# Combining the last expert blocks' outputs on the chip, with the rows of all other blocks read back while those blocks are still computed

## The reference

```
h2 = rmsnorm(x1)
coarse top-1 of 4 groups, then top-2 of 8 experts in it   -> two experts per token, weights w1, w2
y_k = (silu(h2 @ Wg[e_k]) * (h2 @ Wu[e_k])) @ Wd[e_k]      for k = 0, 1;  32 experts, hidden width 256
x  = x1 + w1*y_0 + w2*y_1
out = rmsnorm(x) * g_final
```

## Time and profile before

| | |
|---|---|
| median of 3 runs | 539.98 us |
| the profiled execution | 540.91 us |
| its span in the profile | 539.0 us |
| TensorE busy | 483.3 us (90%) |
| VectorE busy | 237.7 us (44%) |
| GpSimd busy | 183.3 us (34%) |
| ScalarE busy | 100.4 us (19%) |
| mean granted TensorE clock | 0.977 |
| read from HBM, written to HBM | 134.47 MB, 13.17 MB |

### The profile page before, as it was taken

How to read it: one execution, slowest core, us unless ns; L and a number is a source line. 1 busy time by engine, 2 the same in 40 slices (tenths; PEclk the granted TensorE clock), 3 DMA queues, 4 the chain that set the end, 5 groups by cost and what they waited for, 6 DMA issues and landing times.

```text
span 539.0 us, 8928 instructions
## 1 busy us (share of the span) xinstructions
PE 483.3 (90%) x3301; PEld 285.3 (53%) x3302; DVE 237.7 (44%) x514; ACT 100.4 (19%) x204; POOL 183.3 (34%) x282
## 2 busy tenths in 40 slices
PE   6999999999999999999679998989898982998884
PEld 3787777777777545545334443444443441443331
DVE  4219999999964422245821222222122210221246
ACT  5131011002104423324301111101111110011223
POOL 3010817647394600111234443333443332234101
PEclk9989999999999999999789999999999996999999
DMA  8995006100000597023959799999999999999477
GB/s 328 310 391 142 0 2 258 54 2 0 1 1 1 189 412 315 39 69 124 403 192 420 284 411 422 402 397 421 419 418 419 417 419 420 420 418 421 195 272 256
DMA packets 35509, 141.25 MB, mean 262 GB/s; under 512 B 10080, under 2 KB 10096, under 8 KB 23193
## 3 DMA queue, kind: packets, MB, share of 16 engines
q1 hardware_dynamic: 29194, 127.91, 60.4%
q0 software_dynamic: 4960, 9.45, 4.7%
q10 hardware_dynamic: 1327, 3.49, 1.8%
HBM read 134.47 MB, written 13.17 MB: 274 GB/s over the span
## 4 chain that ended last, share of the span: by engine, by line
PE 71%; DMA 12%; DVE 5%; issue 5%; SPq 3%; ACT 2%; POOL 1%; DVEq 0%; POOLq 0%; ACTq 0%
PE bank L1284 26%; PE bank L1367 10%; PE bank L1485 9%; PE bank L1505 8%; PE bank L1480 8%; DMA region_x<-in_w_up 5%; DMA region_w<-in_w_in 3%; PE bank L1277 2%; DMA slot<-y_rows 2%; SPq L402 2%; PE bank L1495 2%; PE bank L1433 1%; DVE ua L1169 1%; PE bank L1393 1%; DVE ua L1171 1%
## 5 line engine op out<-in xcount | busy, mean ns | idle before, releaser
L1284 PE MATMUL bank<-region_h,region_w 128*128 128x256 f32 (+1 forms) x576 | 142.3, 409 | 0.0
L1284 PEld LDWEIGHTS bank<-region_h,region_w 128*128 128x128 f32 x576 | 110.2, 192 | 30.5 <-issue 0.8
L1169 DVE TENSOR_TENSOR ua<-ua,bank 128x128 f32<-128x128 f32 x30 | 8.7, 288 | 174.2 <-ACT ua L639 174.2
L1367 PE MATMUL bank<-region_w,z 128*128 128x512 f32 x128 | 56.7, 596 | 0.2 <-ACT z L584 0.2
L1505 PE MATMUL bank<-region_w,ua 128*32 128x512 f32 x328 | 50.3, 598 | 3.3 <-DVE ua L1171 3.3
L928 DVE SCALAR_TENSOR_TENSOR z<-ub,par,z 128x512 f32<-128x512 f32 x60 | 48.7, 812 | 0.0
L928 DVE SCALAR_TENSOR_TENSOR region_x<-ub,par,region_x 128x512 f32<-128x512 f32 x56 | 45.9, 820 | 0.0
L1485 PE MATMUL bank<-region_w,z 128*32 128x256 f32 x512 | 45.1, 403 | 0.2 <-issue 0.2
L792 POOL COPY gcol<-gidx 128x1 uint32 (+1 forms) x30 | 5.4, 180 | 108.9 <-DVE sb_rows L1158 108.9
L723 POOL TENSOR_TENSOR ub<-region_x 128x512 f32<-128x512 f32 x4 | 20.2, 5056 | 63.8 <-ACT ub L538 32.6
L1485 PE MATMUL bank<-slot,z 128*32 128x256 f32 x192 | 25.9, 425 | 14.5 <-DMA region_w<-in_w_up 9.9
(11 more groups left out here) (244 smaller groups left out, 647.5 us busy)
## 6 DMA issues: line engine op xcount, KB each, us to landing
region_w<-in_w_down SPq DMA_DIRECT2D x21, 1024.0 KB
region_w<-in_w_gate SPq DMA_DIRECT2D x16, 1024.0 KB
region_w<-in_w_up SPq DMA_DIRECT2D x16, 1024.0 KB, 15.7
region_w<-in_w_in SPq DMA_DIRECT2D x4, 2048.0 KB, 19.5
slot<-in_w_gate SPq DMA_DIRECT2D x6, 1024.0 KB, 14.8
slot<-in_w_up SPq DMA_DIRECT2D x6, 1024.0 KB
slot<-in_w_down SPq DMA_DIRECT2D x6, 1024.0 KB
region_x<-in_w_up SPq DMA_DIRECT2D x5, 1024.0 KB
```

What stands on the lines that cost most here:

```text
L1284: ins = mm(ps[2 * bank + j][:, 0:LEN[j]], sec[name][:, k, c * P:(c + 1) * P], hT[:, k, CUT[j]], start=(k == 0), stop=(k == KC - 1))
L1367: ins = mm(ps[2 * (t % 2) + j][0:n, :], z[:, k, t * P:t * P + n], w_out_sb[:, k, j * 512:(j + 1) * 512], start=(k == order[0]), stop=(k == ...
```

## The change

- `y_rows` is filled with zeros by one DMA from a zeroed tile, in SP's queue behind the input weights; the loads of expert 0's gate and up move behind it and behind the router weights.
- `x1` is also stored to a new HBM tensor `x1_rows` (5 stores in SP's queue during the output projection), and the combination weights, transposed by TensorE, to `w_rows` (4 small DMAs of ScalarE).
- The last two blocks are not scattered. Their y stays in the two buffers `yblk`.
- SP no longer waits for all scatters before it loads `y_rows`: it waits for the scatters of all blocks but the last two, and for expert 27's last block (its slot, 3, and slot 2 now receive y). All tiles are then combined with what is there, tiles 1, 3 and 4 on TensorE and tiles 0 and 2 on VectorE, normalized and stored. Rows of the last two blocks' tokens are incomplete in this pass (a zero stands for their missing y).
- These at most 128 tokens are done a second time: GpSimd gathers their `x1` rows (`late`) and the y of their other expert (`other`), TensorE adds both and the two `yblk` buffers (each times a matrix of weights that routes rows to tokens, `same[b]`) in PSUM, ScalarE and VectorE normalize, and GpSimd scatters the rows over those in the outputs, after all plain stores have landed.
- The small tables for this (`vlast`, `ilast`, `dtok`) are computed on VectorE ahead of the block loop, the three gathers of weights (`wlate`) and the matrices `same`, `dother` around the last block. `keep_busy(24)` becomes 8 + 16 with the transpose between them; `keep_busy(32, 1)` is gone. For tiles on TensorE, ScalarE now takes 1024 columns at once, and GpSimd's part in their norm is gone.

The diff, cut to its core:

```diff
-BY_PE = (1, 3)
-
-FINISH = (0, 2, 1, 4, 3)
+BY_PE = (1, 3, 4)
+
+FINISH = (0, 1, 2, 3, 4)
...
+        x1_dram = nc.dram_tensor("x1_rows", (NTOK, D), fp32, kind="Internal").ap()
+
+        w_dram = nc.dram_tensor("w_rows", (2 * NTOK, 1), fp32, kind="Internal").ap()
...
-        yg = [[(SLOT0 if k == 0 else RW)[:, t * D:(t + 1) * D] for t in range(NT)] for k in range(2)]
+        zero = SLOT0[:, 0:D]
+
+
+        free = [RW[:, 2 * SEC + 3 * PART:2 * SEC + 6 * PART], RW[:, 0:3 * PART]]
+        yg = [[free[k][:, t * D:(t + 1) * D] for t in range(NT)] for k in range(2)]
+        late, other = [free[k][:, NT * D:(NT + 1) * D] for k in range(2)]
+        junk = z_t[:, 0:D]
...
+        FREE = 28
+        assert (FREE - 1) % NSLOT == 3 and FREE + NSLOT > NE
...
+        sums = [two_banks[2], two_banks[3], two_banks[1], two_banks[0]]
...
-            for part in range(2):
-                load_part(0, part, 0)
-
+
+            sp.wait_ge(s_zero, 1)
+            sp.dma_start(y_dram.rearrange("(i p) d -> p i d", p=P),
+                         zero.unsqueeze(1).to_broadcast([P, 2 * NTOK // P, D])).then_inc(s_yz, 16)
...
+            sp.wait_ge(s_yz, 16)
+            for part in range(2):
+                load_part(0, part, 0)
...
+            def store_x1(t):
+                sp.wait_ge(s_x1, 2 * t + 2)
+                sp.dma_start(x1_dram[t * P:t * P + TROWS[t], :], x1[0:TROWS[t], t, :]).then_inc(s_x1d, 16)
+
+            for t in range(NT - 1):
+                store_x1(t)
+
             sp.wait_ge(s_o, NT)
             load_expert(3, 3)
+            store_x1(NT - 1)
...
-            pairs = sp.value_load(bound[0:1, PAIRS:PAIRS + 1], min_val=NPAIR // 2, max_val=NBLK // 2)
+
+            lastp = sp.value_load(bound[0:1, LASTP:LASTP + 1], min_val=NPAIR // 2 - 1, max_val=NBLK // 2 - 1)
             odd = sp.value_load(bound[0:1, ODD:ODD + 1], min_val=0, max_val=1)
-            sp.wait_ge(s_ysc[1], pairs * 16)
-            sp.wait_ge(s_ysc[0], (pairs + odd) * 16)
-
-            for t, k in ((0, 0), (0, 1), (2, 0), (1, 0), (2, 1), (1, 1), (4, 0), (4, 1), (3, 0), (3, 1)):
-                sp.dma_start(yg[k][t][0:TROWS[t], :], y_dram[k * NTOK + t * P:k * NTOK + t * P + TROWS[t], :])\
-                  .then_inc(s_yg[k][t], 16)
+            done = sp.value_load(bound[0:1, FREE:FREE + 1], min_val=1, max_val=NBLK)
+            sp.wait_ge(s_ysc[1], lastp * 16)
+            sp.wait_ge(s_ysc[0], (lastp + odd) * 16)
+            sp.wait_ge(s_down, done)
+            for t in range(NT):
+                for k in range(2):
+                    sp.dma_start(yg[k][t][0:TROWS[t], :], y_dram[k * NTOK + t * P:k * NTOK + t * P + TROWS[t], :])\
+                      .then_inc(s_yg[k][t], 16)
...
+            act.wait_ge(s_wT, 1)
+            for k in range(2):
+                act.dma_start(w_dram[k * NTOK:k * NTOK + SEQ, :].rearrange("(t p) o -> t (p o)", p=P),
+                              wT[k * NT:(k + 1) * NT - 1, :]).then_inc(s_wd, 16)
+                act.dma_start(w_dram[k * NTOK + SEQ:(k + 1) * NTOK, :].rearrange("(t p) o -> t (p o)", t=1),
+                              wT[(k + 1) * NT - 1:(k + 1) * NT, 0:TROWS[NT - 1]]).then_inc(s_wd, 16)
...
+                if t == NT or t in BY_PE:
+                    i = len(BY_PE) if t == NT else BY_PE.index(t)
                     act.wait_ge(s_comb, i + 1)
-                    nc.scalar.activation(yg[0][t][:, 512:D], ps[5 + 2 * i][:, :], ACT.Square,
-                                         accum_out=small[:, 8 + t:9 + t]).then_inc(s_sqhalf, 1)
-                    nc.scalar.activation(yg[0][t][:, 0:512], ps[4 + 2 * i][:, :], ACT.Square,
-                                         accum_out=small[:, 16 + t:17 + t]).then_inc(s_sq3, 1)
-
-                    act.wait_ge(s_sq3, at + 1)
-                    act.wait_ge(s_eps3, i + 1)
-                    nc.scalar.activation(small[:, 40 + t:41 + t], small[:, 16 + t:17 + t], ACT.Sqrt,
-                                         scale=1.0 / D, bias=small[:, 48 + t:49 + t]).then_inc(s_rms3, 1)
-                    continue
-                act.wait_ge(s_fin, t // 2 + 1)
-                nc.scalar.activation(yg[0][t][0:n, :], x1[0:n, t, :], ACT.Square,
+                    src = sums[i][0:n, :]
+                else:
+                    act.wait_ge(s_fin, t // 2 + 1)
+                    src = x1[0:n, t, :]
+                nc.scalar.activation(junk[0:n, :], src, ACT.Square,
                                      accum_out=small[0:n, 16 + t:17 + t]).then_inc(s_sq3, 1)
...
+            pool.memset(zero, 0.0).then_inc(s_zero, 1)
...
+            pool.wait_ge(s_ilast, 7)
+            pool.wait_ge(s_wd, 64)
+            for i in range(3):
+                pool.indirect_dma_start(wlate[:, i:i + 1], None, w_dram[:, :],
+                                        bass.IndirectOffsetOnAxis(ap=ilast[:, 4 + i:5 + i], axis=0),
+                                        bounds_check=2 * NTOK - 1, oob_is_err=False).then_inc(s_wg, 16)
+            lastp = pool.value_load(bound[0:1, LASTP:LASTP + 1], min_val=NPAIR // 2 - 1, max_val=NBLK // 2 - 1)
+            done = pool.value_load(bound[0:1, FREE:FREE + 1], min_val=1, max_val=NBLK)
+            pool.wait_ge(s_x1d, 16 * NT)
+            for i in range(2):
+                pool.wait_ge(s_wexp[i][2], 16 * (NE // NSLOT + 1))
+
+            pool.wait_ge(s_yg[1][2], 16)
+            pool.wait_ge(s_down, done)
+            pool.wait_ge(s_ysc[1], lastp * 16)
+            pool.wait_ge(s_ysc[0], (lastp + odd) * 16)
+            pool.tensor_tensor(carry[:, 4:5], carry[:, 1:2], carry[:, 1:2], ALU.add)
+            pool.indirect_dma_start(late, None, x1_dram[:, :], bass.IndirectOffsetOnAxis(ap=ilast[:, 0:1], axis=0),
+                                    bounds_check=NTOK - 1, oob_is_err=True).then_inc(s_late, 16)
+            pool.indirect_dma_start(other, None, y_dram[:, :], bass.IndirectOffsetOnAxis(ap=ilast[:, 1:2], axis=0),
+                                    bounds_check=2 * NTOK - 1, oob_is_err=True).then_inc(s_late, 16)
+
+
+            pool.wait_ge(s_out, 16 * NT)
+            pool.wait_ge(s_nlate, 1)
+            for i, (dst, rows) in enumerate(((y_prompt[0], SEQ), (y_sample.rearrange("s l d -> (s l) d"), NS * SL))):
+                pool.indirect_dma_start(dst, bass.IndirectOffsetOnAxis(ap=ilast[:, 2 + i:3 + i], axis=0), late, None,
+                                        bounds_check=rows - 1, oob_is_err=False).then_inc(s_olate[i], 16)
...
-            link(nc.vector.tensor_tensor(w12[:, NT:2 * NT], w12[:, 0:NT], dlt, ALU.mult))
+            nc.vector.tensor_tensor(w12[:, NT:2 * NT], w12[:, 0:NT], dlt, ALU.mult).then_inc(s_w12, 1)
+            dve.wait_ge(s_wT_ps, 1)
+            nc.vector.tensor_copy(wT, ps[6][0:2 * NT, 0:P]).then_inc(s_wT, 1)
...
+                    nc.vector.tensor_scalar(diag[i][k], ident[0:n, 0:n], w12[0:n, k * NT + t:k * NT + t + 1], None,
...
+            dve.wait_ge(s_yc, 1)
+            even, uneven = pairs * 2 + odd * 2 - 2, pairs * 2 - 1
+            nc.vector.tensor_copy(vlast[:, 0:1], sidx[:, bass.ds(even, 1)])
+            nc.vector.tensor_copy(vlast[:, 1:2], sidx[:, bass.ds(uneven, 1)])
+            nc.vector.tensor_copy(vlast[0:T, 2:3], sidx[0:T, bass.ds(even, 1)])
+            link(nc.vector.tensor_copy(vlast[T:P, 2:3], sidx[T:P, bass.ds(uneven, 1)]))
...
+            nc.vector.tensor_scalar(dtok, ident[:, :], token, float(DA), ALU.mult, ALU.mult).then_inc(s_dtok, 1)
...
+            dve.wait_ge(s_trow, 1)
+            dve.wait_ge(s_wg, 48)
+            for b in range(2):
+                nc.vector.tensor_scalar(same[b], ps[6][:, 0:P], vlast[:, 3 + b:4 + b], wlate[:, b:b + 1],
+                                        ALU.is_equal, ALU.mult).then_inc(s_same, 1)
+            nc.vector.tensor_scalar(dother, ident[:, :], wlate[:, 2:3], None, ALU.mult).then_inc(s_same, 1)
...
-            keep_busy(24)
+            keep_busy(8)
+            pe.wait_ge(s_w12, 1)
+            tr(ps[6][0:2 * NT, 0:P], w12, ident[:, :]).then_inc(s_wT_ps, 1)
+            keep_busy(16)
...
+            pe.wait_ge(s_dtok, 1)
+            mm(ps[6][:, 0:P], lnmean[:, :], dtok, start=True, stop=True).then_inc(s_trow, 1)
...
+                if i == 1:
+                    pe.wait_ge(s_same, 3)
+                if i == 2:
+                    pe.wait_ge(s_yc, pairs * 2 + odd + 1)
+                    mm(sums[i][0:32, 0:1], onesb[:, 0:32], onesb[:, 0:1], start=True, stop=True)
                 for j in range(2):
-                    mm(ps[4 + 2 * i + j][:, :], ident[:, :], x1[:, t, j * 512:(j + 1) * 512], start=True, stop=False)
-            keep_busy(32, 1)
-            for i, t in enumerate(BY_PE):
+                    mm(sums[i][0:n, j * 512:(j + 1) * 512], ident[0:n, 0:n], x1[0:n, t, j * 512:(j + 1) * 512],
+                       start=True, stop=False)
                 for k in range(2):
                     pe.wait_ge(s_yg[k][t], 16)
                     for j in range(2):
```

(38 more changed lines are left out.)

80 lines of the change are left out of this document (45 added, 35 removed).

## The result

The changed kernel takes 551.83 us (median of 4 runs, 549.29 to 554.11), the kernel before 539.82 us beside it (537.75 to 540.32): ratio 1.0229, 95% interval 1.0171 to 1.0286. The prediction was 534.7, faster, with a range of 530.8 to 538.8. It was wrong in sign. The profiled execution took 553.13 us, its span is 551.1. Times here are medians and ratios of executions in the fast state; two far from all others (2699 us in e4, 823 us in the kernel before beside e9 to e12) are left out.

The account below looks back on a forecast made before the run. Bound by scatter, load, combine in series at the end. Loads 10.1 us earlier, half given back: 532.9, plus 0.6 front and 0.2 waits, 533.7, 5.3 below 539.0; 539.98 - 5.3 = 534.7, range 530.8 to 538.8.

Parts of the forecast that it names:

- What bounds the kernel now: End of kernel: scatter, load, combine in series, 27.2 us, with some 10 us of idle DMA ahead of y's loads.
- The front: Start through block 0: zeros, x1 stores and tables nearly all hidden; +0.6 us, for tile 4's x1 store.
- When y can be loaded: SP's queue: block 27's scatter lands about 504.0, first y load at 504.1 instead of 514.24, 10.1 us earlier.
- The engines at the end: Combining the tiles: VectorE and loads set the pace, two 0.46 us matmuls per y load; TensorE finishes tile 4 by 519.9.
- Rival (4): Combine at the end: TensorE at 1.2 GHz, 26 matmuls at 0.93 us, late sum to 534.6, median 543.9; chance 0.05.
- The late rows: Second pass for the last two blocks' tokens: gathers landed 521.5, 8 matmuls of 3.7 us, late sum done 525.2.
- rival (1): Late path: gathers and scatters slower under load, late rows at 523.6, scatters 1 us more; +3, 537.7; chance 0.15.
- Behind the late sum: From late sum at 525.2: ScalarE 526.7, VectorE 528.3, scatters landed 532.4, end 532.9 before front and Pool waits.

Follow-up runs that it names:

- e4: Kernel after without late gathers, late sum, its norm and late scatters (a probe, result incomplete): 536.24 us, ratio to the kernel before 0.9966.
- e9: Kernel after with combine calls on 256 columns, not 512 (half not summed), plus bf16 filler matmuls ahead of TensorE's waits: 546.67 us, ratio to the kernel before 1.0121.
- e12: Kernel before with only the change's front (zeros, order of first loads, stores of x1): ratio to the kernel before 1.0000.
- e1: Kernel after with tile 4's sum put back on VectorE: 552.33 us, ratio to the kernel before 1.0270.
- e6: Kernel before with one small GpSimd memset at the end, waiting for the last tile's norm: ratio to the kernel before 1.0049.
- e2: Kernel after with the four products of yblk done ahead of tile 1's sum: 546.55 us, ratio to the kernel before 1.0170.
- e5: Kernel after with every combine call on 256 columns in place of 512, half not summed: 551.18 us, ratio to the kernel before 1.0218.
- e7: Kernel before with norms of TensorE's tiles 1024 columns wide, without two small GpSimd instructions: ratio to the kernel before 0.9994.
- e11: Kernel after with e1 and e2, ident products early, late gathers right after block 27's y, late sum before tile 3, tile 4 before 3: 546.26 us, ratio 1.0107.

## Why the prediction was wrong

**What bounds the kernel now, The front, When y can be loaded**: right. The scatter of block 27 landed at 504.14 (504.0 forecast), the first load was issued at 504.30. The idle 10 us of DMA were there to be had. The landings were not: the first came at 507.82 (507.7 forecast), the next five 1.7 to 2.5 late, tile 3's second y at 521.84 (517.5) and tile 4's at 523.02 (518.9). Each load lands in 16 parts. The last part was late; the first parts kept a pace of 1.3 us, near the forecast 1.4. From the first issue to the last landing the ten loads took 18.7 us, 15.8 in the kernel before. The late gathers are not the cause: in e4, without them, it is 18.8. SP's ten loads took, from issue to landing (min/median/max), in the kernel after and then in the kernel before:

```profile
DMA to landing us min/median/max: 3.5/9.1/13.3
```

```profile
DMA to landing us min/median/max: 3.5/8.0/11.1
```

**The engines at the end: the step that failed.** I wrote "two matmuls of 0.46 per y load, from 3.70 for 8". The row is right and the reading wrong: its 8 instructions are 4 calls, two tiles by two halves, as the loop at L1557 says. A y load is two calls and four instructions, 1.86 us. The Trainium skill, "FP8 and Floating Point Precision", section "TensorE Precision Notes", has true fp32 go through the array four times; an estimate from that is 4 x 512 columns at 2.4 GHz, 0.85 us a call, and the trace agrees, with 0.86 to 0.93. So the combine was never "VectorE and the loads set this": 26 calls are 24 us of TensorE. Tile 3 was done at 525.9 (518.5 forecast), tile 4 at 531.3 (519.9). Rival (4) had this price, "26 matmuls at 0.93 us", and I gave it 0.05, since I took 0.93 for the price at 1.2 GHz. It is the price at 2.4. Its condition, the end at 1.2 GHz, did not come about, so the rival was near for a wrong reason; its late sum ended at 534.6, 4.5 too early, by the late y and the clock.

**The late rows.** Forecast 525.2, measured 539.1, 13.9 us later, and the parts add up: both gathers had landed at 528.8 and not 521.5, 7.3; TensorE reached them 2.5 later, at 531.3; 16 instructions took 7.8 with the one before them and not 3.7, 4.1. Of the 2.5, 1.7 is the clock in 520 to 525. The gathers are the second term that was too small: the first was issued at 518.57 (515.4 forecast), and from there to the landing of both it took 10.2 us and not 6.1; rival (1) had them at 523.6. The two errors hide each other. With gathers on time TensorE would still have come at 531.3 and ended at 539.1; with the forecast's TensorE, the gathers alone would have put the end at 532.5 (528.8 and 3.7). e1 shows the same from the other side: without the 2.5 the gathers decide, and the clock gives most of the time back. In e9, with the work that the forecast charged and the clock held, the late sum ended 21.9 us after the copy in place of 28.7; the forecast, 525.2, is 14.7 after it in the kernel before. So TensorE's price and its clock are worth 6.8 us, and of the 7.2 that are left 6.5 are the gathers' (17.5 us after the copy, 11.0 by the forecast's 521.5).

**Behind the late sum.** Forecast 7.9 us, measured 12.0. ScalarE, VectorE and the scatters were near their prices (scatters 2.3 to 2.6 from issue to landing), and 4.1 is the drain, for which there was no term. The kernel before had its drain level with SP's end (538.8 both), so its cost was invisible, and "the kernel ends when the last store has landed" held there only just. e6 shows that a later last instruction of GpSimd moves the end; in the kernel after SP was through at 546.9, 4.0 ahead of the drain's end. With these 13.9 and 4.1 more, and the front's 0.6 less, the forecast's 533.7 becomes the span of 551.1.

**What was really on offer.** Half of it I had seen: that the late part is a second combination in series. e4 puts the gain from the early loads at 1.8 us (0 to 3.6 by its interval) even with no late part at all, since TensorE's three tiles are then what ends last (its sum of tile 4 ends at 529.35, the last store lands at 535.2, the span at 535.7). The change pays 13.7 us for it. The 1.8 is no bound on what early loads can give: e4 with tile 4 on VectorE and the clock held was not run.

Open: why the runs of e2 and e9 fall into two groups of mean clock; why the clock stayed low in e5 beside a busy TensorE; and what spreads the landings of the last y loads (with e4, not the late gathers).

## What to carry to other kernels

Divide the xN of a profile's matmul group by the calls in the source before taking a price from it; fp32 is two instructions a call here. Check what stands level with the end (GpSimd's drain, a second wait) before you make the last step one of GpSimd's, and ask of every wait that you add on TensorE what clock the work behind it will get. Where a wait is for two DMAs, read the landing of the second. An early start is worth only what the engines behind it have spare: sum their work from the first start to the end first.

## What the runs showed of the hardware

- GpSimd's closing drain ended 5.2 us after its last instruction behind small operations (e6, and the kernel before) and behind a scatter (e7), 5.6 behind the two late scatters, 6.75 behind three gathers beside the weights (e4). Where it ends last, it holds the end of the kernel.
- Two gathers of 0.5 MB beside loads of y and stores took 9.6 us (e2) to 14.5 us (e11) from the first issue to the landing of both.
- With gaps, halving the columns of TensorE's calls brought nothing: the granted clock went to 0.50 behind a gap of 3.76 us and stayed there for the 15 us of nearly dense matmuls of 256 columns that followed (e5); with fillers in the gaps it stayed at 1.00 (e9).
- fp32 matmuls on partitions 0 to 63 and 64 to 127 issued next to each other overlap: 8 in 1.99 us, 3.96 when apart (e2).
- A half-row scatter issued while the weight queue is full took 6.75 us, 2.27 once it was empty.
